# Reordering three places of a hybrid two-block stack: a gate product, memory scores in two steps, context rows turned earlier

## The reference, cut to what matters

```python
s = jnp.einsum('bthd,bnhd->bhtn', q, k) * (MEM_HEAD_DIM ** -0.5)   # memory attention, A and B
p = jax.nn.softmax(s, axis=-1)
...
h = _rms(x, g_pre) * (1.0 + scale) + shift                          # second block, each layer
hc = _rms(xc, g_pre) * (1.0 + mod_c[1]) + mod_c[0]                  # context rows
na_k, na_v, df_k, df_v, na_q, na_g, df_q, df_g, cv_a, cv_b, cv_g = _split_cols(h @ w_in, ...)
a_out = neighbourhood attention;  b_out = difference of two softmaxes, (p1 - lam * p2) @ v
y = concat(...) @ w_out;  x = x + gate * _rms(y, g_post)
```

## Time and profile before

| | |
|---|---|
| median of 3 runs | 1653.34 us (1653.3 to 1657.56) |
| the profiled execution's own time | 1653.44 us |
| its span in the profile | 1651.6 us |
| PE busy | 1597.0 us, 97% |
| DVE busy | 979.8 us, 59% |
| ACT busy | 667.6 us, 40% |
| POOL busy | 140.7 us, 9% |
| chain that ended last | PE 83%, DVE 10%, ACT 4%, issue 2% |

### The profile page before, as it was taken

The page is one execution under the profiler, slowest core; times in us unless marked ns, Lnnn a source line. Parts: engine busy times, 40 slices in busy tenths (PEclk is TensorE's granted clock), DMA queues, the critical chain, the costliest instruction groups (busy, mean ns, idle before and its releaser), DMA issues.

```text
span 1651.6 us, 22948 instructions
## 1 busy us (share of the span) xinstructions
PE 1597.0 (97%) x8870; PEld 1277.7 (77%) x8870; DVE 979.8 (59%) x1803; ACT 667.6 (40%) x1323; POOL 140.7 (9%) x192
## 2 busy tenths in 40 slices
PE   7999999899999999999999999989999999999898
PEld 6977877687878878878888888865656887788676
DVE  1356454456556655665447787565665467876674
ACT  3365443424323323263313435244554325433653
POOL 4132100000000000002000110000112001000001
PEclk9999999899999999999999999999999999999899
DMA  8221244334654764462223111221003134213100
GB/s 289 81 77 50 103 153 117 80 82 121 190 158 120 155 185 139 148 151 68 92 96 109 56 54 40 92 93 58 1 26 96 48 107 140 58 39 128 52 14 39
DMA packets 171252, 161.36 MB, mean 98 GB/s; under 512 B 40374, under 2 KB 154280, under 8 KB 171112
## 3 DMA queue, kind: packets, MB, share of 16 engines
q1 hardware_dynamic: 151944, 126.97, 26.1%
q10 hardware_dynamic: 16928, 25.27, 4.7%
q0 software_dynamic: 2272, 7.64, 1.4%
HBM read 149.80 MB, written 11.18 MB: 97 GB/s over the span
## 4 chain that ended last, share of the span: by engine, by line
PE 83%; DVE 10%; ACT 4%; issue 2%; DMA 0%; POOL 0%; ACTq 0%; SPq 0%; POOLq 0%; DVEq 0%
PE psum L2596 46%; PE psum L2567 10%; PE psum L2630 7%; PE psum L3139 5%; PE psum L2621 4%; PE psum L3137 2%; PE psum L2775 2%; PE psum L2687 2%; PE psum L2730 2%; DVE arena L1999 1%; PE psum L2669 1%; PE psum L3010 1%; DVE arena L1969 1%; DVE wring_r L2076 1%; DVE arena L2133 1%
## 5 line engine op out<-in xcount | busy, mean ns | idle before, releaser
L2596 PE MATMUL psum<-hT_r,wring_r 128*128 128x512 f32 x1696 | 575.2, 393 | 3.6 <-ACT branch L1745 1.1
L2596 PEld LDWEIGHTS psum<-hT_r,wring_r 128*128 128x128 f32 x1696 | 319.3, 188 | 79.0 <-issue 10.0
L2596 PE MATMUL psum<-arena_r,wring_r 128*128 128x256 f32 (+1 forms) x1360 | 359.1, 333 | 0.7 <-ACT branch L1564 0.5
L1564 ACT ACTIVATE arena<-psum 128x512 f32<-128x512 f32 (+6 forms) x256 | 149.8, 611 | 416.0 <-PE psum L2596 244.2
L2596 PEld LDWEIGHTS psum<-arena_r,wring_r 128*128 128x128 f32 x1360 | 218.3, 190 | 26.2 <-issue 1.8
L2567 PE MATMUL psum<-arena 128*128 128x96 f32 (+9 forms) x1460 | 220.8, 365 | 16.9 <-ACT branch L1745 7.1
L2596 PE MATMUL psum<-arena_r 128*128 128x512 f32 (+1 forms) x720 | 224.5, 350 | 0.0
L2567 PEld LDWEIGHTS psum<-arena 128*128 128x128 f32 (+5 forms) x1460 | 160.8, 189 | 64.7 <-issue 31.9
L2596 PE MATMUL psum<-hT_r,arena_r 128*128 128x512 f32 x448 | 177.8, 397 | 1.8 <-DVE wring_r L2076 1.0
L2630 PE MATMUL psum<-ident,arena 128*128 128x128 f32 (+3 forms) x1104 | 145.9, 277 | 17.4 <-DMA arena<-in_c_ctx 7.4
L2630 PEld LDWEIGHTS psum<-ident,arena 128*128 128x128 f32 (+3 forms) x1104 | 125.2, 142 | 39.6 <-issue 14.6
(11 more groups left out here) (237 smaller groups left out, 1967.8 us busy)
## 6 DMA issues: line engine op xcount, KB each, us to landing
wring<-in_w_in_b SPq DMA_DIRECT2D x54, 512.0 KB, 5.9
arena<-in_w_mod ACTq DMA_DIRECT2D x16, 1536.0 KB, 8.3
wring<-in_w_in SPq DMA_DIRECT2D x16, 1536.0 KB, 6.9
wring<-in_w_out SPq DMA_DIRECT2D x8, 2048.0 KB, 8.4
wring<-in_w_in_a SPq DMA_DIRECT2D x5, 1536.0 KB, 6.6
arena<-x_dram SPq DMA_DIRECT2D x3, 2048.0 KB, 14.6
wring<-in_w_in SPq DMA_DIRECT2D x6, 1024.0 KB, 5.7
arena<-ebias_dram SPq DMA_DIRECT2D x144, 32.0 KB, 1.8
```

The lines of the kernel that those rows point to most:

```text
L1564: return nc.scalar.activation(out, in_, ACT.Copy, scale=scale)
L2596: ins_ = nc.tensor.matmul(b[0:hi.shape[2], 0:width], w[:, k], v[:, k], start=k + p == 0, stop=(k, p) == (KT - 1, 2))
```

## The change

The list of steps is changed in four places. `mem_jobs` is new; it gives the jobs of a score step, and PE, ACT and DVE number their banks within the step.

1. Layer A: the eight score jobs become two steps of four, gate 6 after the first and gate 7 after the second.
2. Layer B: gate 4 stands ahead of the memory queries and no longer behind them. The list of chunks is as before. The rule that places splits now puts split 26 ahead of `qm`, and split 27 behind `mS`.
3. Layer 1 of the second block: `nv` stands ahead of `nq`.
4. Layer 0 of the second block: `hcT` 1 stands ahead of `dPV` of the last item but one, and no longer behind `doT` of the last tile.

```diff
@@ schedule()
-    add("a" * 8, "mS", "A")
-    add("a", "gate", "A", 6)
-    add("a", "gate", "A", 7)
+    for part in range(2):
+        add("a" * 4, "mS", "A", part)
+        add("a", "gate", "A", 6 + part)
...
-    for i in range(4):
+    for i in range(5):
         add("a", "gate", "B", i)
     add("av", "qm", "B")
-    add("a", "gate", "B", 4)
-    add("a" * 8, "mS", "B")
+    add("a" * 8, "mS", "B", 0)
...
-        add(lat_ctx * 3, "nq", l)
+        if l == 0:
+            add(lat_ctx * 3, "nq", l)
         add("aaaavv", "nv", l)
+        if l:
+            add(lat_ctx * 3, "nq", l)
         neighbourhood(add, l)
...
+def mem_jobs(key):
+
+    return range(8) if key[1] == "B" else range(4 * key[2], 4 * key[2] + 4)
@@ diff_stage()
             if todo:
                 project()
+            if n == len(items) and l == 0:
+                add("vvvv", "hcT", 1)
             if h == 0 and i:
                 add("v", "doT", l, tiles[i - 1])
...
     add("v", "doT", l, last)
-    if l == 0:
-        add("vvvv", "hcT", 1)
-    else:
+    if l:
         add("", "yx", l, before)
...
-        split_starts = [("wout", "A"), ("wout", "B"), ("hcT", 1)]
+        split_starts = [("wout", "A"), ("wout", "B"), ("doT", 0, TT - 1)]
@@ DVE, step mS
+                    jobs = mem_jobs(key)
+
                     def mem_normalise(i):
-                        evacuated(dve, key, i)
+                        evacuated(dve, key, i - jobs[0])
...
-                    for i in range(8):
-                        b = full(dve, key, i)
+                    for i in jobs:
+                        b = full(dve, key, i - jobs[0])
...
-                        if i:
+                        if i > jobs[0]:
                             mem_normalise(i - 1)
-                    mem_normalise(7)
+                    mem_normalise(jobs[-1])
```

More of the change, by code:

```diff
@@ L1749, in _ @@
                     ph = "AB".index(key[1])
-                    for i in range(8):
-                        b = bank(key, i)
+                    for j_, i in enumerate(mem_jobs(key)):
+                        b = bank(key, j_)
                         act.wait_ge(mem_negmax, 8 * ph + i + 1)
@@ L2838, in _ @@
                     evacuated(pe, ("qm", ph), 1)
-                    for i in range(8):
+                    for i in mem_jobs(key):
                         t, odd = divmod(i, 2)
                         lo = odd * MD
-                        b = claim(pe, key, i)
+                        b = claim(pe, key, i - mem_jobs(key)[0])
                         for j in range(2):
```

## The result

The changed kernel takes 1655.49 us (median of 20 runs, 1650.94 to 1658.3), the kernel before, timed beside it, 1652.68 (20 runs). The ratio is 1.0016, 95% interval 1.0009 to 1.0022: 2.6 us slower, 1.5 to 3.6, within what was called no change. The profiled execution took 1657.37 us with a span of 1655.6, which is 4.0 more than the span before. Among all runs reported here one execution, of 1799.45 us in the run with POOL's additions earlier, showed a granted clock of 0.845 over its whole span; it is left out of that run's ratio.

What follows compares the result with a forecast made beforehand. PE, busy 97% of the span, was taken to bound the kernel. Minus 10.0 + 2.0 - 0.8 + 10.8 = plus 2.0 us on 1653.44, itself 0.1 above the median, gave 1655.3, range 1648 to 1661.

Steps and rivals of the forecast that it cites:

- no change: Whole kernel: a time from 1648.4 to 1658.3 us, since a measurement tells 0.3%, 5.0 us; chance 0.65.
- The signs that it named: Layer B: ACT's split wait about 7 us; layer A: `mPV` 1 to 3 later; layer 0's end: PE hole about 7.6.
- The new wait: Layer B, ahead of the scores: gate 4 no longer covers DVE's copy of the second query bank; 0.8 us charged.
- 0.7 for the low clock: Layer A: value products, 3.67 us, may run at the low clock, nothing to 3.7 us more; 0.7 taken.
- bound of plus 5.0: Layer A: upper bound on its cost, which was put at plus 2.0 us, with minus 1.0 as lower bound.
- that rival: Layer A: a table change costs 2.66 us, giving some 2.8 us more and 1658.1 in all; chance 0.03.
- the list of what moves with the values: Layer 1: POOL's mask additions fall behind its value write, SP's 16 strip reads pass the last gates' chunk; edit minus 0.8 us.
- cost nothing: Layer 1: POOL's three mask additions, now behind its value write, are first needed behind 72 query products and half a gate.
- the low clock was put at 2.0: End of layer 0: after PE idles 7.6 us the low clock costs 2.0 us, taken out of 3.0.
- the 0.85: End of layer 0: time back where the context transposes stood, 1.2 us in place of 2.07, so minus 0.85.
- lower bound: Context rows: plus 8.2 us, counting at most 0.5 back as layer 1's first context keys no longer wait for DVE.
- The rival in which they are hidden: End of layer 0: context rows cost no hole and give minus 0.85 us; sum minus 9.6, 1643.7; chance 0.12.

Runs made afterwards that it cites:

- the seam alone: Kernel before with layer A's memory scores in two steps of four, gates 6 and 7 both behind the second, table changes as before: 1653.28 us, ratio 0.9998.

## Why the prediction was right, and where it was not

The forecast was 1655.3 with 0.65 on no change; 1655.49 was measured. The signs that it named came: ACT waited 6.99 us at the split of layer B, layer A's value products stood 1.4 later, and PE's hole at the end of layer 0 was 7.56 us, with DVE's 16 operations in it. By its terms:

| part | predicted | in the trace | alone |
|---|---|---|---|
| layer B | -10.0 | -10.7 | -10.9 |
| layer A | +2.0 | +4.2 | +2.6 |
| layer 1 | -0.8 | +0.1 | -0.8 |
| context rows | +10.8 | +10.7 | +9.1 |
| between the edits | 0 | -0.3 | |
| sum | +2.0 | +4.0 | measured together: +2.6 |

- **Layer B: right.** The new wait was put at 0.8 and is 0.83. Chunk 1 was to land at 301.5, in the changed kernel's time 305.8; its split began at 306.43, and the query copy was done 0.8 us before PE's 168 products, where 1.3 was foreseen. The score products were charged 4.3 and took 3.8. The moved gate is one way; moving the split is another, as large.
- **Layer A: mechanism right, one term mis-sized.** The last exponential was to end at 209.75, and the load behind it starts at 209.97; the value products were to start at 213.7 and start at 213.88. The term "0.7 for the low clock" was 2.9 (6.54 less 3.67), still in the bound of plus 5.0. I had argued that PE is only nearly idle there; two short turns of 0.63 us between three waits (0.46, 1.28, 1.24) did not keep the clock up. A load of 1.28 had no further drain: in all three the next activation starts 0.02 after its end, so the Trainium skill's 1.38 ("ScalarE: Activation LUTs", "What ACT_TABLE_LOAD costs") is not seen here, and that rival falls.
- **Layer 1: a step failed.** The gain came out at 1.2 at the first scores, and 1.3 was lost behind them. What failed is the list of what moves with the values: I took SP's 16 strip reads to pass only a weight chunk, but the bias transfers stood behind them. These began 5.5 us earlier against the first scores, and POOL's next addition fell on DVE's normalising: 0.99 of wait. The sentence that POOL's three additions "cost nothing" held for PE alone. I asked who needs their result and not what they run beside, and they held DVE up by 4.0 us, which it made good before PE asked. The Trainium skill, page "SBUF — State Buffer", section "Who interferes with whom", says that a DVE instruction with two SBUF inputs contends with a GpSimd instruction that reads SBUF. The trace agrees: two splits took 6.38 us beside the additions, 2.35 without them.
- **Context rows: right.** The last turn was to be 9.6 late and is 9.5 (+2.6 after -6.8); the low clock was put at 2.0 and is 2.4 (from that turn to the `yo` of 20 products 8.4 us, where it was 6.0); back came 0.8 of the 0.85, and 0.4 more at the first context keys, which the forecast had in its lower bound alone. The rival in which they are hidden falls.
- **The near hit has luck in it.** Between the two profiled executions the difference is +4.0, twice the sum: layer A is 2.2 and layer 1 0.9 above its term, and layer B, the context rows and the rest are 1.1 below. The 20 timed runs of each kernel give +2.6. The two profiled executions took 0.8 and 1.9 us more than the medians beside them (1652.68 and 1655.49), which is within the 7 to 8 us that single executions of either kernel lie apart; more was not traced. One such place is known: the wait ahead of the fourth scores of layer 1 was 0.70, 1.74 and 2.20 us in the kernel before, the one with layer A's scores alone and the one with the seam alone, though layer 1 is the same in all three.

## What to carry to other kernels

A moved step moves on every engine's queue: ask on each what stands right behind it and who waits for that, on DVE and POOL also what will run beside it, and on the DMA queue which transfers stood behind it and now come early. The biggest gain here was a weight split that waited on its transfer ahead of a short activation that PE needed; placing the split later gave as much as fetching the weights earlier. In layer A 1.4 us more of wait on PE came with 2.9 us more in the clock behind it, so work that keeps PE busy can be worth more than the wait alone, and a reorder that adds changes of ACT's table must be followed job by job to the product that waits.

## What the runs showed of the hardware

- A DVE instruction of 1.2 us with both inputs in SBUF stood for all three of POOL's additions (4.0 us lost beside 3.80 us of POOL), not for one of them. The kernel with the values alone has the same (6.39), and the two kernels with the additions earlier have 2.35. Two DVE multiplications by a column of factors, with one tensor input in SBUF, took 1.90 us beside one addition of 1.33, and 0.88 without it.
- The low clock came behind short waits. In the changed kernel, with waits of 0.46, 1.28 and 1.24 us between turns of 0.63 each, the granted clock was 0.57 from 212 to 220; in the kernel with the seam alone, with one wait of 1.15, it was 1.00 in the same window. In the first case PE had made only 32 turns in the 7.0 us before (206.86 to 213.88), in the second the same 32 in 4.8 us (208.12 to 212.93); what of this counts, no run here tells apart. With the context rows behind the combine, a wait of 2.75 was followed by 0.52 over 3.5 us.
